# A hybrid mixer layer on one core: plain products for the first two pairs, the 31-tap conv in PSUM, a third bank beside branch M

## What is computed

```python
proj = x @ w_in[l]                       # 1024 x 1024 by 1024 x 8200, columns split among the branches
a_u, a_v = jnp.split(a_glu, 2, axis=-1)  # 512 columns each
a = _causal_dwconv(a_u * jax.nn.sigmoid(a_v), conv_a_w[l]) + conv_a_b[l]      # 31 taps, 512 channels
a = jax.nn.silu(_layer_norm(a, ln_a_g[l], ln_a_b[l]))
y_a = (a * jax.nn.silu(a_gate)) @ p_a[l]
hb = b_b * _causal_dwconv(b_c * b_h, conv_b_w[l])                             # 3 taps
y_b = (hb * jax.nn.silu(b_gate)) @ p_b[l]
y_c = (o_c * jax.nn.silu(c_gate)) @ p_c[l]      # o_c: forgetting attention, 8 heads
y_m = (o_m * jax.nn.silu(m_gate)) @ p_m[l]      # o_m: attention into 256 memory tokens, 4 heads
gates = jax.nn.sigmoid(g.reshape(bsz, seq, N_BRANCH, D_MODEL))
merged = gates[:, :, 0] * y_a + gates[:, :, 1] * y_b + gates[:, :, 2] * y_c + gates[:, :, 3] * y_m
x = _layer_norm(ALPHA * x + merged @ w_out[l], ln_g[l], ln_b[l])
```

## Time and profile before

| | us |
|---|---|
| median of three runs | 1318.26 |
| lowest, highest | 1317.86, 1320.16 |
| the profiled execution's own time | 1321.32 |
| its span, first to last instruction | 1319.5 |
| busy: PE / DVE / POOL / ACT | 1234.6 / 886.0 / 769.4 / 545.4 |
| PE at: first matmul, pair 2, pair 24, end of pairs | 8.15, 68.35, 520.10, 644.94 |

### The profile page before, as it was taken

How to read it: one execution, slowest core, us unless ns; L and a number is a source line. 1 busy time by engine, 2 the same in 40 slices (tenths; PEclk the granted TensorE clock), 3 DMA queues, 4 the chain that set the end, 5 groups by cost and what they waited for, 6 DMA issues and landing times.

```text
span 1319.5 us, 16434 instructions
## 1 busy us (share of the span) xinstructions
PE 1234.6 (94%) x5704; PEld 1009.8 (77%) x5704; DVE 886.0 (67%) x1199; ACT 545.4 (41%) x1000; POOL 769.4 (58%) x528
## 2 busy tenths in 40 slices
PE   6799999999999999999999999999998889899997
PEld 4588788777777777788888878778787777678886
DVE  4615876797697796427777666767667466766864
ACT  4443333332423433557335555645545334314200
POOL 6888989999999999878503132132321224446200
PEclk8799999998999999999999999999999999999999
DMA  6121221222222223323602111111002423247332
GB/s 193 55 62 44 64 72 57 64 97 96 98 94 96 96 98 119 104 97 96 223 2 81 49 49 48 32 48 48 24 10 89 164 97 107 92 152 275 98 126 80
DMA packets 92132, 118.49 MB, mean 90 GB/s; under 512 B 5912, under 2 KB 73496, under 8 KB 92064
## 3 DMA queue, kind: packets, MB, share of 16 engines
q1 hardware_dynamic: 92064, 117.60, 27.2%
HBM read 92.39 MB, written 25.20 MB: 89 GB/s over the span
## 4 chain that ended last, share of the span: by engine, by line
PE 45%; POOL 25%; DVE 9%; issue 5%; ACT 3%; DMA 0%; DVEq 0%; ACTq 0%; POOLq 0%; SPq 0%
POOL ring_lo L1476 15%; POOL w_pair L1504 7%; PE pj L734 4%; PE pj L735 4%; PE pj L736 4%; PE pj L982 3%; PE pj L751 3%; PE pj L753 2%; PE pj L752 2%; PE pj L695 2%; PE pj L697 2%; PE pj L696 2%; POOL s_w L1504 2%; PE po L843 2%; PE pt L830 2%
## 5 line engine op out<-in xcount | busy, mean ns | idle before, releaser
L1476 POOL TENSOR_TENSOR ring_lo<-w_pair,ring_hi 128x512 fp32r<-128x512 f32 x180 | 310.7, 1740 | 43.9 <-ACT ring_hi L1040 43.8
L1685 DVE SCALAR_TENSOR_TENSOR slot<-glu,cwa,slot 128x1024 f32<-128x1024 f32 x116 | 234.1, 2054 | 24.5 <-ACT slot L1092 24.5
L1545 POOL TENSOR_TENSOR w_lo<-w_raw,w_hi 128x128 fp32r<-128x128 f32 (+1 forms) x104 | 107.3, 1051 | 243.5 <-ACT w_hi L1135 241.3
L1040 ACT ACTIVATE ring_hi<-w_pair 128x512 fp32r<-128x512 f32 x180 | 110.5, 626 | 225.4 <-POOL w_pair L1504 178.4
L695 PE MATMUL pj<-t_hi,ring_hi 128*128 128x512 f32 x420 | 168.5, 401 | 25.4 <-POOL ring_lo L1476 10.7
L696 PE MATMUL pj<-t_lo,ring_hi 128*128 128x512 f32 x420 | 166.5, 396 | 0.0
L697 PE MATMUL pj<-t_hi,ring_lo 128*128 128x512 f32 x420 | 166.4, 396 | 0.0
L734 PE MATMUL pj<-xT_hi,w_hi 128*128 128x512 f32 x320 | 126.4, 395 | 0.0
L735 PE MATMUL pj<-xT_lo,w_hi 128*128 128x512 f32 x320 | 125.4, 392 | 0.0
L736 PE MATMUL pj<-xT_hi,w_lo 128*128 128x512 f32 x320 | 125.0, 391 | 0.0
L695 PEld LDWEIGHTS pj<-t_hi,ring_hi 128*128 128x128 f32 x420 | 80.6, 192 | 49.7 <-issue 12.7
(11 more groups left out here) (273 smaller groups left out, 2927.2 us busy)
## 6 DMA issues: line engine op xcount, KB each, us to landing
w_pair<-in_w_in SPq DMA_DIRECT2D x28, 1024.0 KB, 5.2
gate_scratch<-slot SPq DMA_DIRECT2D x16, 1024.0 KB, 4.0
gate<-gate_scratch SPq DMA_DIRECT2D x32, 512.0 KB, 3.6
w_raw<-in_w_in SPq DMA_DIRECT2D x20, 512.0 KB, 3.9
z_scratch<-slot SPq DMA_DIRECT2D x8, 512.0 KB, 2.7
bias<-cum_scratch SPq DMA_DIRECT2D x8, 512.0 KB, 3.7
wout_raw<-in_w_out SPq DMA_DIRECT2D x8, 512.0 KB, 5.8
x_tok<-in_x SPq DMA_DIRECT2D x8, 512.0 KB, 4.4
```

The costliest lines, as they stand in the source:

```text
L1040: nc.scalar.activation(ring_hi[:, j % RING, :, :], w_src(u, p), ACT.Copy).then_inc(s_rhi, 1)
L1476: nc.gpsimd.tensor_tensor(ring_lo[:, j % RING, :, :], w_src(u, p), ring_hi[:, j % RING, :, :], ALU.subtract).then_inc(s_rlo, 1)
L1545: nc.gpsimd.tensor_tensor(w_lo[:, j % 2, k, :], w_raw[:, j % 2, k, :], w_hi[:, j % 2, k, :], ALU.subtract).then_inc(s_wlo, 1)
L1685: nc.vector.scalar_tensor_tensor(out=acc, in0=glu[:, ct, n:n + T], scalar=cwa[:, ct, n:n + 1], in1=acc, op0=ALU.mult, op1=ALU.add).then_in ...
```

## The change

1. *First two pairs.* `SEQ` now begins with pair 2. Pairs 0 and 1 are computed plainly before it: eight groups g, one PSUM bank each (all eight banks), 8 k-steps of 3 matmuls per group, in the order of x halves (first half of x for the four column tiles, then the second). Their weights' hi and lo parts are eight entries in the ring's space and three more. Tanh and GLU read the banks directly (`first_tanh`, `first_glu`). The sums, copies and results of pairs 0 and 1 go. The t blocks are still made, a little later. SP's loads of pairs 2 and 3 wait for the fourth and the eighth lo part.
2. *Conv.* The accumulator is `po`, banks 6 and 7, one per half of the columns. ACT writes tap 0 with the bias (two operations of 512 columns), DVE adds the taps 1 to 30 to each half in turn (60 steps of 512 columns per channel tile); the last one writes to `glu` in SBUF.
3. *Beside branch M.* The halves take banks 0, 1 and 7 in turn (`m_bank`). `mweigh` writes both heads to bank 6; ACT's two shifts wait for both (`m_shift`), DVE's two adds for both shifts. The tiles behind that stage exchange their two sets of banks.

```diff
-    SEQ = [(0, 1), (0, 2), (1, 1), (1, 2), (0, 5), (1, 5), (0, 6), (0, 7), (0, 3), (1, 6), (0, 4), (1, 7), (1, 3),
-           (1, 4)] + [(u, p) for u in range(2, NP) for p in ORDER]
+    SEQ = [(u, p) for u in range(2, NP) for p in ORDER]
...
-        count = (4, 4, 4, 4, 4, 4, 3, 3, 8, 8, 7, 7, 8, 8, 7, 7, 8, 8, 7, 7)[u - 4]
+        count = (8, 8, 8, 8, 8, 8, 6, 6, 16, 16, 14, 14, 16, 16, 14, 14, 16, 16, 14, 14)[u - 4]
...
+    CONV_OPS = 2 * (CONV_A - 1)
...
+        def m_bank(s, h):
+            return (0, 1, 7)[(2 * (s - S_M) + h) % 3]
...
             def load_pair(u):
-                if u >= 2:
+                if u < 4:
+                    sp.wait_ge(s_elo, 4 * (u - 1))
+                else:
                     sp.wait_ge(s_rlo, max(SLOT_OF[u - 2, p] for p in ORDER) + 1)
...
+            for g in range(8):
+                u, n, h = g // 2 % 2, g % 2, g // 4
+                for k in range(KT):
+                    e = 4 * u + 2 * n + k // KH
+                    if h == 0 and k % KH == 0:
+                        pe.wait_ge(s_elo, e + 1)
+                    if g == 0 and k in (0, 2, KH):
+                        pe.wait_ge(s_xbl, k // 2 + 1)
+                    if g == 4 and k % KH == 0:
+                        pe.wait_ge(s_xbl, 4 + k // KH)
+                    w_h, w_l = first_w(e)
+                    nc.tensor.matmul(bank(g), w_h[:, k % KH, :], xT_hi[:, h, k, :], start=k == 0, stop=False)
+                    nc.tensor.matmul(bank(g), w_h[:, k % KH, :], xT_lo[:, h, k, :], start=False, stop=False)
+                    mm = nc.tensor.matmul(bank(g), w_l[:, k % KH, :], xT_hi[:, h, k, :], start=False, stop=k == KT - 1)
+                mm.then_inc(s_grp, 1)
...
                 for s, h, k, nk in M_FILL[n0:n1]:
-                    if k == 0:
+                    if k == 0 and s == S_M:
                         pe.wait_ge(s_pjfree, 2 * s + h - 1)
+                    elif k == 0 and s == S_M + 1 and h == 0:
+                        pe.wait_ge(s_oadd, PV_PAIR * CT)
+                    elif k == 0:
+                        pe.wait_ge(s_pjfree, 2 * s + h - 2)
...
                 pe.wait_ge(s_tlo, TB + 2 * g + 2)
+                pe.wait_ge(s_oadd, PV + 2 * g)
                 for a in range(2):
-                    pe.wait_ge(s_oadd, PV + 2 * g + a - 1)
...
-                                po[:, a, 0:2 * P],
+                                po[:, 0, a * 2 * P:(a + 1) * 2 * P],
...
                 if j >= RING:
                     act.wait_ge(s_prod, j - RING + 1)
+                else:
+                    act.wait_ge(s_grp, 5 + j // 2)
...
-                nc.scalar.activation(slot[2][:, 0, :], glu[:, ct, 0:T], ACT.Identity, scale=cwa[:, ct, 0:1],
-                                     bias=cab[:, ct:ct + 1]).then_inc(s_conv0, 1)
-                nc.scalar.activation(slot[2][:, 1, :], glu[:, ct, 1:1 + T], ACT.Identity,
-                                     scale=cwa[:, ct, 1:2]).then_inc(s_conv0, 1)
+                for h in range(2):
+                    nc.scalar.activation(po[:, h, :], glu[:, ct, h * HALF:(h + 1) * HALF], ACT.Identity,
+                                         scale=cwa[:, ct, 0:1], bias=cab[:, ct:ct + 1]).then_inc(s_conv0, 1)
...
+            def m_shift(g):
+
+                act.wait_ge(s_pv, PV + 2 * g + 2)
+                act.wait_ge(s_oadd, PV + 2 * g)
+                for a in range(2):
+                    b, o = DH * a, DH * (1 - a)
+                    nc.scalar.activation(otmp[b:b + DH, :], po[o:o + DH, 0, a * 2 * P:(a + 1) * 2 * P],
+                                         ACT.Copy).then_inc(s_osh, 1)
...
             def conv_op(ct, k):
 
-                acc = slot[2][:, k % 2, :]
-                if k < CONV_A - 2:
-                    n = k + 2
-                    if k < 2:
-                        dve.wait_ge(s_conv0, 2 * ct + k + 1)
-                    else:
-                        dve.wait_ge(s_conv, 30 * ct + k - 1)
-                    nc.vector.scalar_tensor_tensor(out=acc, in0=glu[:, ct, n:n + T], scalar=cwa[:, ct, n:n + 1], in1=acc,
-                                                   op0=ALU.mult, op1=ALU.add).then_inc(s_conv, 1)
+                n, h = 1 + k // 2, k % 2 if k < CONV_OPS - 2 else 1 - k % 2
+                acc = po[:, h, :]
+                src = glu[:, ct, n + h * HALF:n + (h + 1) * HALF]
+                if k < 2:
+                    dve.wait_ge(s_conv0, 2 * ct + h + 1)
+                elif k < CONV_OPS - 2:
+                    dve.wait_ge(s_conv, CONV_OPS * ct + k - 1)
                 else:
-                    dve.wait_ge(s_conv, 30 * ct + k)
-                    nc.vector.tensor_tensor(glu[:, ct, PAD_A:WA], slot[2][:, 0, :], slot[2][:, 1, :],
-                                            ALU.add).then_inc(s_conv, 1)
+                    dve.wait_ge(s_conv, CONV_OPS * ct + k)
+                nc.vector.scalar_tensor_tensor(out=acc if n < PAD_A else src, in0=src, scalar=cwa[:, ct, n:n + 1], in1=acc,
+                                               op0=ALU.mult, op1=ALU.add).then_inc(s_conv, 1)
```

More of the change, by code:

```diff
@@ L75, in hybrid_mixer @@
     COPY_NO, SUM_NO, TANH_NO = {}, {}, {}
-    for up in [(0, 1), (1, 1), (0, 5), (0, 6), (1, 5), (1, 6)] + [(u, p) for u in range(2, NP) for p in (1, 5, 6)]:
+    for up in [(u, p) for u in range(2, NP) for p in (1, 5, 6)]:
         COPY_NO[up] = len(COPY_NO) + 1
@@ L284, in hybrid_mixer @@
         s_wp0 = {n: sem(f"w_first_pair_loaded_{n}") for n in ("11", "12", "2")}
-        s_wp1 = sem("w_second_pair_half_loaded")
+        s_wp1 = [sem(f"w_second_pair_loaded{n}") for n in range(2)]
+        s_ehi = sem("first_w_hi_made")
+        s_elo = sem("first_w_lo_made")
+        s_grp = sem("first_half_accumulated")
+        s_tanh0 = sem("first_tanh_made")
         s_wp = [sem(f"w_pair_loaded{i}") for i in range(2)]
@@ L646, in _, with first_w, first_src @@
                 sp.wait_ge(s_store[i], 16 * (NT // 2 + i))
+        def first_w(e):
+            if e < RING:
+                return ring_hi[:, e, :, :], ring_lo[:, e, :, :]
+            return first_hi[e - RING][:, :, :], first_lo[e - RING][:, :, :]
+        def first_src(e):
+            k0, c0 = e % 2 * KH, e // 2 % 2 * P
+            return w_pair[e // 4][:, k0:k0 + KH, c0:c0 + P]
         @block.tensor
@@ L750, in p_steps @@
                         pe.wait_ge(s_zl, z0 + k + 1)
-                    nc.tensor.matmul(pj[:, bank, :], w_hi[:, s % 2, k, :], hi[k][:, hs(h)], start=k == 0, stop=False)
-                    nc.tensor.matmul(pj[:, bank, :], w_hi[:, s % 2, k, :], lo[k][:, hs(h)], start=False, stop=False)
-                    mm = nc.tensor.matmul(pj[:, bank, :], w_lo[:, s % 2, k, :], hi[k][:, hs(h)], start=False,
+                    nc.tensor.matmul(bank(b), w_hi[:, s % 2, k, :], hi[k][:, hs(h)], start=k == 0, stop=False)
+                    nc.tensor.matmul(bank(b), w_hi[:, s % 2, k, :], lo[k][:, hs(h)], start=False, stop=False)
+                    mm = nc.tensor.matmul(bank(b), w_lo[:, s % 2, k, :], hi[k][:, hs(h)], start=False,
                                           stop=k == nk - 1)
@@ L1135, in split_w, with first_hi_make, first_tanh @@
                     nc.scalar.activation(w_hi[:, j % 2, k, :], w_raw[:, j % 2, k, :], ACT.Copy).then_inc(s_whi, 1)
+            def first_hi_make(e):
+                if e < 4:
+                    act.wait_ge(s_wp0[("11", "12", "2", "2")[e]], 16)
+                else:
+                    act.wait_ge(s_wp1[e // 2 % 2], 16)
+                nc.scalar.activation(first_w(e)[0], first_src(e), ACT.Copy).then_inc(s_ehi, 1)
+            def first_tanh(g):
+                act.wait_ge(s_grp, g + 1)
+                nc.scalar.activation(slot[0][:, g % 2, g // 4 * HALF:(g // 4 + 1) * HALF], bank(g), ACT.Tanh,
+                                     scale=0.5).then_inc(s_tanh0, 1)
@@ L1149, in _ @@
[L1149 to L1152, removed]
+            first_hi_make(2)
+            first_hi_make(3)
+            act.wait_ge(s_xr["12"], 16)
+            x_hi(4, xT_hi[:, 1, 0:KH, :], r12[:, :, :])
+            for e in range(4, 8):
+                first_hi_make(e)
+            act.wait_ge(s_xr["22"], 16)
+            x_hi(5, xT_hi[:, 1, KH:KT, :], r22[:, :, :])
+            first_tanh(0)
+            act.wait_ge(s_xbt, 1)
+            x_hi(6, t_hi[0][:, :, :], r11[:, :, :])
@@ L1181, in _ @@
+            first_tanh(1)
+            act.wait_ge(s_xbt, 4)
+            act.wait_ge(s_xbl, 5)
+            x_hi(9, t_hi[3][:, :, :], r21[:, :, :])
+            first_tanh(4)
+            w_hi_make(0)
+            w_hi_make(1)
+            first_tanh(5)
+            for j in range(2, RING):
+                w_hi_make(j)
             for u in range(2, NP):
@@ L1412, in _ @@
                 if w % 2 == 0 and w:
-                    for a in range(2):
-                        out_shift(a, a, PV + w - 2 + a)
+                    m_shift(w // 2 - 1)
                 if w in (2, 3):
@@ L1436, in _ @@
             mturned_hi(2 * NT - 1)
```

(18 more changed lines are left out.)

219 lines of the change are left out of this document (83 added, 136 removed).

## The result

The changed kernel takes 1252.68 us (median of 4 runs, 1250.63 to 1253.82) against 1318.06 for the kernel before: ratio 0.950, 95% interval 0.948 to 0.952. The forecast was 1256, its range 1249 to 1271. The profiled executions differ by 1319.5 - 1251.4 = 68.1 us of span, the medians by 65.4: the kernel before was profiled in an execution 3 us above its median.

The account below looks back on a forecast made before the run. PE, busy 94%, was taken as the bound, losing time to waits for POOL and DVE and to clock dips. Terms 9.05 + 31.4 + 2.6 + 19.5 = 62.5 us off 1318.26 gave 1255.8, said 1256; range 1249 to 1271.

Parts of the forecast that it names:

- First two pairs: Start of the kernel: computed plainly, pairs 0 and 1 end at 59.3 us instead of 68.35, -9.05 us.
- Conv: Pairs 2 to 29: PSUM accumulator frees POOL, pairs run at 19.04 us; -31.4 us to pair 23, -2.6 after.
- The one reserve, 1.5 us for pair 6: Pair 6: four short-conv taps stay in SBUF, so 1.5 us of PE's 2.6 us wait was kept.
- The row from which the prediction read that POOL is quiet beside a PSUM input: Timeline before: POOL's operation takes 1.29 us while DVE runs L1651 (one PSUM operand), 2.28 beside L1685.
- Beside branch M: Stage beside branch M: a third bank gives each half 2.7 us more time before evacuation, -19.5 us.
- 2.4 us for the longer chain: Stage beside branch M: 2.4 us left for later adds on DVE and the z_lo steps in two rounds.
- wait for pT_lo, kept at 1.7 us: End of the stage beside branch M: 1.7 of 5.9 us clock loss left to a wait that stays.
- A: Beside branch M: DVE's chain sets the pace, half of the 19.5 us is gone, 1266 us; chance 0.17.
- B: Pairs 2 to 29: POOL stays stretched by steps writing PSUM, 28.5 us left, 1290 us; chance 0.07.
- C: First stage: gives nothing, weight parts late and PE back at half clock, 1265 us; chance 0.07.
- D: Conv pairs: DVE becomes the bound and the kernel slower, 1340 us at 1.6 us a step; chance 0.04.
- Its threshold: Conv pairs: beyond (19.04 - 2.1) / 15 = 1.13 us a step, DVE sets the pace.

Follow-up runs that it names:

- Run 3: The kernel before with only the plain first two pairs, conv and branch M stage as before: 1310.25 us.
- run 1: The kernel before with only the conv accumulator moved to PSUM: 1282.98 us, ratio 0.972.
- run 2: The changed kernel with the conv of before (two accumulators of 1024 columns in SBUF): 1287.65 us.
- run 4: The changed kernel with its 240 conv steps of 512 columns kept but the accumulator back in SBUF: 1303.86 us.
- run 8: The changed kernel with two banks for the halves beside branch M, but the new weigh in one bank and both shifts before both adds: 1274.75 us.
- run 6: The changed kernel with a second DVE operation of the same shape, writing SBUF, before each conv step: 1281.77 us.
- run 7: The changed kernel with the stage beside branch M as before (two banks, heads in two banks, shift and add in turn): 1273.53 us.
- run 5: The changed kernel with 120 conv steps of 1024 columns, one accumulator across both PSUM banks: 1252.32 us.

## Why the prediction was right

*First two pairs* (-9.05, measured -9.80). The groups run one behind the other at 5.43 to 5.45 us from 20.45 us on, as worked out. POOL's fifth lo part began at 18.71 us (18.7 had been given) and the eighth was done by 31.49 (at the latest 32.1, needed at 34.8). The 0.75 us more came from the clock. The twelve matmuls behind the wait for xT_lo start at about the same time in both (16.06 us, and 15.95 before), but full pace is back at 19.5 us instead of 21.5: the window has 0.86 where before had 0.75. Run 3 has the whole term alone.

*Conv* (-31.4 and -2.6, measured -32.9 and -2.9). The chain of reasons held: the step reads 748 ns (0.69 taken, 0.63 to 1.03 as bounds), POOL is held no more, the pairs run at PE's pace. DVE itself is busy for 248.75 us in pairs 2 to 23 instead of 331.84. Runs 1, 2 and 4 show that the accumulator's place does this, not the halves and not the new start. The one reserve, 1.5 us for pair 6, was not needed: PE has no wait there.

The row from which the prediction read that POOL is quiet beside a PSUM input did not show it cleanly. L1651 ends 0.34 us into that POOL operation of 1.29 us (259.66); the rest of it ran beside another DVE operation:

```profile
260.04 1.47 DVE L1796 TENSOR_TENSOR slot<-slot,slot 128x512 f32<-128x512 f32 x1
```

This one has two SBUF inputs, and here it was DVE's operation that was stretched (the same one, L1830 in the changed kernel, takes 0.69 us in the row above). What the prediction read from the row came true, but it is the runs that show it.

*Beside branch M* (-19.5, measured -23.1). Mechanism right, reserve too large. I had left 2.4 us for the longer chain and for DVE's lag behind the z_lo steps; the waits came to 0.8 us, and run 8 shows no price of the chain beyond 0.3, within what runs differ by. The clock lost nothing there (1.00 in the window). The half-clock stretch behind the wait for pT_lo, kept at 1.7 us in this stage, falls behind its end in this execution (0.66 over the first 5 us of the tail), while before it lay half on each side. So part of the 3.6 us beyond the forecast only moved across the line, and is in the +0.6 of the tail.

*The rivals.* A (DVE's chain takes over) is refused by the stage itself: DVE's wait for otmp fell to 7.7 us, and PE's waits did not move elsewhere. B (POOL stays stretched) is refused by the timelines and run 1. C by run 3. D is real as a mechanism: run 6 produces it, and run 4 shows a second way into it. Its threshold was worked out with the length of an operation and not with the distance of starts. With it, it is (19.04 - 1.8) / 15 = 1.15 us between starts, in lengths a good 1.2; that is an estimate, since no run has a load between 0.66 and 1.26 us for each step of 512 columns in PSUM.

The parts add up, each taken against the kernel before on its own chip: 36.7 us for the conv part alone (1319.72 - 1282.98) and 9.5 for the first stage alone are the 46.2 of run 7, which has both. The banks were not run alone; for them remains what the whole gains (65.4, and 66.9 where it was timed again) less these 46.2, so 19.2 to 20.7. The stage's own windows give the banks 22.9 us (149.35 - 126.41). In the two profiled executions the difference lies in the tail, 163.7 us in the changed kernel and 160.9 in run 7: the changed kernel has its half-clock stretch there (0.66 over 5 us, 1.7 us lost), run 7 at the same place 1.00.

## What to carry to other kernels

When two engines that are both off the critical path stretch each other's operations, price the pair by the timelines: here one operand's place decided over 36 us. Look for a row in which the two operations lie beside each other for their whole length; the one used here did not. The idle bank paid where a producer waited for an in-order consumer that is only sometimes late: one more buffer took away waits of up to 2.8 us at no cost of work. Then price a threshold by the distance of starts and not by the length of a row.

## What the runs showed that I had not expected

Two engines that hold each other up do not simply take turns. DVE's timeline of the kernel before has six conv steps on end, beside POOL operations:

```profile
285.60 12.88 DVE L1685 SCALAR_TENSOR_TENSOR slot<-glu,cwa,slot 128x1024 f32<-128x1024 f32 x6
```

The first of them is shorter (1.71 us); the others start 2.23 us apart, and so do POOL's operations beside them. Undisturbed, by the distance of starts again, DVE's step takes 1.19 us and POOL's operation 1.24, 2.43 together. So some 0.2 us of each pair still overlaps. And which engine loses depends on the sizes: with steps of 1024 columns PE waited for POOL and for sums, with steps of 512 in SBUF for DVE's sums alone (run 4).

A conv step with its accumulator in PSUM reads 748 ns and takes 0.66 us from start to start; the sum at the same width that writes SBUF reads 0.69 and takes 0.61. It is not the output in PSUM that costs these 0.05 us. The last step of each half writes SBUF, and has the same length and the same distance to the next operation:

```profile
251.66 0.73 DVE L1721 SCALAR_TENSOR_TENSOR glu<-glu,cwa,po 128x512 f32<-128x512 f32 x1
252.32 0.68 DVE L1843 TENSOR_TENSOR slot<-pj,slot 128x512 f32<-128x512 f32 x1
```

So has the step of run 4, all in SBUF, where POOL left it alone (736 to 747 ns, 0.66 us). At 1024 columns the next operation starts 1.19 us after the step either way, in run 5 as in the kernel before with POOL quiet. What the longer operations have in common is the tap, a factor read from a tensor: L2130, the same kind of operation with a constant factor, reads 682 ns. No run changes that alone.
